# Constant products on TensorE during three waits of a two-layer hybrid decoder kernel

## The reference

```python
h = rmsnorm(x, p['norm_mix_g'])
u = h @ p['w_in']                       # [SSD | RWKV | latent attention] columns
o_ssd  = ssd_mixer(u_ssd, ...)          # convolution, silu, chunked scan
o_rwkv = rwkv_mixer(u_rwkv, ...)        # group-normed scan output, + bonus, * gate
q   = mla_queries(u_mla[..., :512], ...)
ckv = rmsnorm(u_mla[..., 512:768], ...); kpe = rope(u_mla[..., 768:], pos)
o_mla = attend(q, ckv, kpe, p)          # prompt: causal; sample: over a paged cache
merged = gate0*(o_ssd @ w_o_ssd) + gate1*(o_rwkv @ w_o_rwkv) + gate2*(o_mla @ w_o_mla)
x = x + merged @ p['w_out']
x = x + ConvFFN(rmsnorm(x, p['norm_ffn_g']))
```

## Time and profile before

| | |
|---|---|
| median of 3 runs | 3048.22 us (3045.31 to 3050.01) |
| profiled execution | 3045.14 us; span of its instructions 3043.4 us |
| TensorE matmul busy | 2704.4 us (89%), 24160 records |
| VectorE / ScalarE / GpSimd busy | 1898.3 us (62%) / 1353.5 us (44%) / 843.8 us (28%) |
| mean granted TensorE clock | 0.943 of full speed |

### The profile page before, as it was taken

The page is one execution under the profiler, slowest core; times in us unless marked ns, Lnnn a source line. Parts: engine busy times, 40 slices in busy tenths (PEclk is TensorE's granted clock), DMA queues, the critical chain, the costliest instruction groups (busy, mean ns, idle before and its releaser), DMA issues. The chain is left out here.

```text
span 3043.4 us, 62226 instructions
## 1 busy us (share of the span) xinstructions
PE 2704.4 (89%) x24160; PEld 2475.1 (81%) x24160; DVE 1898.3 (62%) x3163; ACT 1353.5 (44%) x2302; POOL 843.8 (28%) x696
## 2 busy tenths in 40 slices
PE   7886777999998889899988868789999888898998
PEld 6876447999987679899978764589999886898998
DVE  4854455777865655489458453567777666554993
ACT  4733343545553343354356333435555442433542
POOL 0030005999940400000000300069999304000000
PEclk9999988999998989999989989789999989999999
DMA  5323328867545276365453233299775453764644
GB/s 132 104 61 106 105 63 135 154 113 141 88 80 156 72 201 165 102 162 145 124 119 91 70 112 99 53 148 152 116 130 84 80 156 95 197 163 109 166 131 126
DMA packets 832231, 365.86 MB, mean 120 GB/s; under 512 B 400045, under 2 KB 819414, under 8 KB 831368
## 3 DMA queue, kind: packets, MB, share of 16 engines
q1 hardware_dynamic: 829714, 360.77, 51.6%
q10 hardware_dynamic: 2232, 1.26, 0.2%
HBM read 342.63 MB, written 61.23 MB: 133 GB/s over the span
## 5 line engine op out<-in xcount | busy, mean ns | idle before, releaser
L1170 PE MATMUL key_banks<-w_kb_head,latent_T_head 128*128 128x352 f32 x1536 | 520.3, 339 | 30.3 <-DVE latent_T_rest L1317 26.4
L1170 PE MATMUL key_banks<-w_kb_rest,latent_T_head 128*128 128x352 f32 x1536 | 496.9, 323 | 0.0
L1170 PE MATMUL key_banks<-w_kb_head,latent_T_rest 128*128 128x352 f32 x1536 | 496.3, 323 | 0.0
L293 DVE TENSOR_TENSOR w_rests<-w_ring,w_heads 128x2048 fp32r<-128x2048 f32 (+1 forms) x152 | 326.3, 2150 | 164.5 <-ACT w_heads L287 164.2
L1170 PEld LDWEIGHTS key_banks<-w_kb_head,latent_T_head 128*128 128x128 f32 x1536 | 291.4, 190 | 44.3 <-issue 28.6
L1331 DVE TENSOR_REDUCE w_kb<-key_sq 128x8 f32<-128x1024 f32 x256 | 310.8, 1214 | 11.8 <-ACT key_sq L1243 7.7
L952 POOL TENSOR_TENSOR rwkv_state_tmp<-rwkv_state,vec 128x1024 f32<-128x1024 f32 x64 | 154.6, 2415 | 529.4 <-DMA rwkv_state<-in_state_rwkv_dram 524.5
L287 ACT CAST w_heads<-w_ring 128x2048 fp32r<-128x2048 f32 (+1 forms) x152 | 272.3, 1794 | 52.9 <-ACT conv_last_rows L1873 19.7
L2789 POOL TENSOR_TENSOR L_level<-L,const 128x1024 f32<-128x1024 f32 x24 | 56.3, 2366 | 856.6 <-DVE L L2795 801.3
L1170 PEld LDWEIGHTS key_banks<-w_kb_rest,latent_T_head 128*128 128x128 f32 x1536 | 291.7, 190 | 0.0
L1170 PEld LDWEIGHTS key_banks<-w_kb_head,latent_T_rest 128*128 128x128 f32 x1536 | 290.4, 189 | 0.0
(11 more groups left out here) (564 smaller groups left out, 7026.5 us busy)
## 6 DMA issues: line engine op xcount, KB each, us to landing
w_ring<-in_ffn_w_up_dram SPq DMA_DIRECT2D x88, 512.0 KB, 5.0
page_latents<-in_cache_kv_latent_dram SPq DMA_DIRECT2D x256, 128.0 KB, 2.4
latent_blocks<-page_latents SPq DMA_DIRECT2D x256, 128.0 KB, 3.8
latents<-page_latents SPq DMA_DIRECT2D x64, 512.0 KB, 8.5
w_ring<-in_w_in_dram SPq DMA_DIRECT2D x52, 512.0 KB, 3.9
w_ring<-in_w_gate_dram SPq DMA_DIRECT2D x48, 512.0 KB, 4.0
w_ring<-in_w_in_dram SPq DMA_DIRECT2D x20, 1024.0 KB, 6.1
w_ring<-in_ffn_w_down_dram SPq DMA_DIRECT2D x32, 384.0 KB, 3.3
```

The source lines that it names most:

```text
L293: ops.tensor_tensor(rests[:, slot, 0:tiles * P], ring[:, slot, 0:tiles * P], heads[:, slot, 0:tiles * P].bitcast(F32), ALU.subtract).then_ ...
L1170: last = nc.tensor.matmul(kbank[:, 3 * x + n, 0:KB], c[:, x, r * P:(r + 1) * P], w[:, r, cols], start=r == 0 and m == 0, stop=r == 1 and m ...
```

## The change

A helper issues `n` plain float32 products of the identity with the first 512 columns of the constants, into a bank of which nobody reads the result. It is called on TensorE in three places of each layer: at the start of `mla_project` (12 products, bank 5), ahead of the last sequence's `TURN_TOP` in `cache_attention` (14 products, key bank 0, after a wait that the scores of the last but one page were copied out), and at the start of `ssd_project` (6 products, bank 7).

```diff
+def idle_products(nc, k, out, n):
+
+    for _ in range(n):
+        nc.tensor.matmul(out, k.col("ident"), k.const[:, 0:BANK], start=True, stop=True, skip_group_check=True)
@@ mla_project, tensor
                     last.then_inc(y_turned, 1)
+                idle_products(nc, k, banks[:, 5, :], 12)
                 for i in range(3):
                     if i:
                         pe.wait_ge(split, i)
@@ cache_attention, tensor
                 def finish(b, slot, at):
                     if at == TURN_TOP:
+                        if is_last(b):
+                            pe.wait_ge(taken, NB * PAGES - 1)
+                            idle_products(nc, k, kbank[:, 0, :], 14)
                         pe.wait_ge(topped, b + 1)
                         nc.tensor.transpose(mbank[0:32, 0:128], top[:, :], k.col("ident")).then_inc(top_turned, 1)
@@ ssd_project, tensor
             def _(pe):
+                idle_products(nc, k, banks[:, 7, :], 6)
                 for u in range(NU):
```

## The result

The changed kernel takes 3053.6 us (median of 22 runs, 3045.0 to 3062.7); the runs of the kernel before beside it have a median of 3044.7 us (22 runs). The ratio is 1.0038, 95% interval 1.0029 to 1.0046: slower by 12 us (9 to 14). It is not the ratio of the two medians, which lie 8.9 us apart. Timed once more later, beside other runs of before, it was 1.0026 (1.0012 to 1.0040), 8 us. Forecast: slower by 8.0 us; the first interval begins just above that, the second holds it. The forecast total of 3056 us was built on the median of three runs of before, 3.5 us above that of the 22, so its closeness to 3053.6 says less than the difference does.

What follows compares the result with a forecast made beforehand. TensorE, busy 89% of the span, was taken as the bound, so its lateness usually delays everybody. Latent projection 0.3, last maxima 7.4 and ssd projection 0.3 gave +8.0 us on the 3048.2 median: 3056 us, range 3047 to 3063.

Steps and rivals of the forecast that it cites:

- The price of a product: Each added 512-column float32 product on TensorE is two records, 0.853 us at full clock and 1.71 us at half.
- Rival 2: An identity product costs one record, 0.427 us, so the products fit the waits: some -7 us, 3041; chance 0.07.
- The lateness of the transpose: Cache attention, last sequence: 14 products outlast the 7.00 us wait, so transpose L1182 starts 4.95 us later per layer, +9.9 us.
- What the clock gives back in the tail: Behind the last sequence's transpose, fuller clock regains 2.5 us over both layers, none of it at L1210; part sum +7.4 us.
- rival 1: Full clock lasts to the end of L1210, which shrinks to 3.5 us: whole -1.0 us, 3047; chance 0.12.
- The latent projection: 12 products at its start: 0.5 and 1.3 us late, -1.55 by `turn_y(0)` at full clock; sum +0.3 us.
- The ssd projection: 6 products at its start: a warm unit 0 gains nothing, small margin before unit 1; +0.3 us, ends 0 and +2.8.
- One sign: Ssd projection: unit 1 still released by VectorE, 15.1 and 14.1 us into the stage.
- Rival 3: The added products don't wake TensorE's clock and run at half: together +57 us, 3105; chance 0.03.
- The sum: Whole kernel: 0.3 + 7.4 + 0.3 = +8.0 us, ends -3.2 and +17.4.

Runs made afterwards that it cites:

- b_8_tail: Against the kernel before: only 8 products ahead of the last sequence's transpose, plus short ones in each of the four waits behind it; ratio 0.9959, 3027.8 us.

## Why the prediction was right, step by step

- *The price of a product, 0.853 us.* Right: two records each; 28 of them took 24.1 us. Rival 2 (one record) is out.
- *The lateness of the transpose, 4.95 us a layer.* Right, 912.48 to 917.47 in the first layer and 12.24 less 7.30 us in all six layers with 14 products. That it is this that costs is shown by the count: 8 products -6.7 us, 14 +7.3, 28 +25.6; by the tails alone -3.1, +5.4 and +28.4.
- *What the clock gives back in the tail, 2.5 us.* Right in size, partly by luck. In the two profiles compared it gave back 3.0, but as +3.4 in the first layer (forecast 1.8; the values took 2.4 us, a gain of 2.1 where I had counted 1.2) and -0.4 in the second (forecast +0.7), where the clock fell during the values while in before it had risen there. Set against the mean of the unchanged tails it is 4.5 in two layers, so the part is +5.4 and not +7.4. L1210 gave back 0.3 us in the first layer and lost 0.3 in the second: rival 1 is out for this kernel. `b_8_tail` shows that its mechanism exists all the same, when TensorE has work in each wait of the chain.
- *The latent projection, +0.3 us.* Right in its stage (+0.1). The terms: -1.55 by `turn_y(0)` at the full clock in the first layer, 0.0 late there instead of 0.5 (block 0 began 11.5 us after the products, since the clock rose sooner than I took), 1.6 late in the second instead of 1.3. But the 1.55 came from one profile: `turn_y(0)` ran at full clock in 8 of the 14 layers without products ahead of it (in the unchanged kernel's second profile it took 2.08 us in the first layer and 2.91 in the second) and took 2.5 us on average, so the clock is worth 0.8 us in two layers, and the stage is nearer +0.9 than +0.1. By the medians the part alone was +7.6 and +4.3, which neither the theory nor a row explains.
- *The ssd projection, +0.3 us.* The stage was 0.8 us shorter in after, and no difference was measured for the part alone; over all profiles the stage is equally long with and without the products (79.3 and 79.2 us a layer). One sign failed: unit 1 was not released by VectorE in the first layer any more: TensorE came 14.6 us into the stage straight from unit 0, VectorE's rests having been earlier than before. The margin was as small as I had it.
- *Rival 3*, products that don't bring the clock: out. The longest record of the latent projection is 1192 ns and the median 592: they begin at half clock and end at full. The Trainium skill ("TensorE: Matmul & The Clock Gate", Part 4: PE-mode transpose), weighed before, does not reach ordinary products with the identity; whether a transpose in its own mode counts, no run here shows.
- *The sum.* +8.0 against +11.6 (9 to 14) and +7.9 (4 to 12). The direction and the largest term, the late transpose, are shown. That the total comes so near is in part luck: the rows of the three stages, each set against the mean of the kernels without the part, add up to +6.4 (5.4, 0.9 and 0.1), and the remaining 5 and 1.5 us of the two measurements stay open. The parts alone were timed at +7.3, +7.6 and +4.3, and +2.7 us, 14 to 18 together, which would more than cover them, but in the stage of the second part no row has its time.

The best version of these runs is `b_8_tail` with 3027.8 us, 0.41% below the kernel before and, by the ratios, 0.7% to 0.8% below the changed one (0.9959 against 1.0026 and 1.0038); the one with products ahead of `turn_y(0)` is equal to it.

## What to carry to other kernels

Work that only keeps TensorE's clock up must end before the wait that it fills is over: price it by a row of the same form at the granted clock of the place (here 0.853 us a product, 8 in a 7.00 us wait), because from there on each product is paid in full by whatever chain hangs on TensorE. Ask also what the clock is for: a warm start bought nothing where another engine releases the next block, and something in a chain of short TensorE steps: 1.5 us a layer with products ahead of the chain alone, 5.3 with products in every wait of it. When many short stretches depend on the clock, compare medians, and stages over several profiles, not two profiles with each other.

## What the runs showed of the hardware

A run of 32 plain float32 records of 32 columns, each behind a load of 128 columns of weights, lost the clock while TensorE was busy 3.00 of 3.00 us (granted 0.50 in 928 to 931 of after). It took 3.8 us where the clock held and 4.8 to 7.0 where it fell on the way or had fallen before, and where it began at half clock it ended there: 7.0 us of it didn't bring the clock back, while twelve 512-column products that began at half clock had it within their 12.1 and 12.9 us. When the clock falls is not fixed by the instructions: rows that were the same to 0.02 us from the last scores on gave 4.88 us in one layer and 3.76 in the other. A stage that nobody touched (`ssd_tiles`, second layer) varied from 71.7 to 79.7 us over fourteen profiles; in the two compared above the granted clock was 0.91 and 0.80 over the same 570 records.
